# The attention branch placed beside the recurrence's last operations, merged quarters transposed between branch units, and a new prologue

## The reference, cut to what matters

```
h      = rms_norm(x)
proj   = h @ w_in                        # q|k|v, z = r|kr|vr + three low-rank (LORA) pieces, two gates
attn   = sliding_window_attention(q, k, v, sinks)          # 16 heads, window 128
z      = z + (token_shift(z) - z) * shift_mix
y      = rwkv7(z ...)                                      # 16 heads, delta-rule state
y      = (group_norm(y) * ln_w + ln_b + bonus) * g
merged = sigmoid(ga) * (attn @ w_branch_a) + sigmoid(gb) * (y @ w_branch_b)
x      = x + merged @ w_out
x      = x + hierarchical_moe(rms_norm(x))   # 32 experts 2048 -> 512 -> 2048, top 2 of one group
out    = rms_norm(x) * final_norm_w
```

## Time and profile before

| | us |
|---|---|
| median of 3 runs | 1893.07 |
| the profiled execution, device time | 1895.63 |
| its span | 1893.8 |
| PE busy / DVE / ACT / POOL | 1454.5 / 487.2 / 342.5 / 31.8 |

### The profile page before, as it was taken

The page is one execution under the profiler, slowest core; times in us unless marked ns, Lnnn a source line. Parts: engine busy times, 40 slices in busy tenths (PEclk is TensorE's granted clock), DMA queues, the critical chain, the costliest instruction groups (busy, mean ns, idle before and its releaser), DMA issues.

```text
span 1893.8 us, 23945 instructions
## 1 busy us (share of the span) xinstructions
PE 1454.5 (77%) x10765; PEld 834.2 (44%) x10765; DVE 487.2 (26%) x614; ACT 342.5 (18%) x396; POOL 31.8 (2%) x23
## 2 busy tenths in 40 slices
PE   5999999999889979899656657566575675856754
PEld 4999974457546748777411212112121131311311
DVE  2454433352343245544201001001010010100102
ACT  2444422212121123334300001000010000100001
POOL 0000000001001000000000000000000000000000
PEclk9999999899979989999888888778887797887976
DMA  7655433241202247545599999999999999999993
GB/s 229 239 188 188 165 108 122 84 146 51 101 8 99 97 162 238 196 155 207 228 422 421 422 422 422 421 422 422 422 422 422 423 421 423 422 422 422 422 422 145
DMA packets 114683, 529.00 MB, mean 279 GB/s; under 512 B 7729, under 2 KB 9883, under 8 KB 64572
## 3 DMA queue, kind: packets, MB, share of 16 engines
q1 hardware_dynamic: 109184, 512.27, 67.8%
q10 hardware_dynamic: 4284, 11.58, 1.8%
q0 software_dynamic: 1152, 4.19, 0.6%
HBM read 521.74 MB, written 6.29 MB: 279 GB/s over the span
## 4 chain that ended last, share of the span: by engine, by line
PE 58%; DMA 32%; DVE 4%; ACT 3%; issue 1%; ACTq 1%; DVEq 0%; SPq 0%
DMA ring<-in_expert_w_down 21%; DMA ring<-in_expert_w_up 11%; PE ps L469 10%; PE ps L521 10%; PE ps L789 9%; PE ps L890 6%; PE ps L907 5%; PE ps L916 3%; PE ps L859 2%; DMA ring<-in_expert_w_gate 1%; PE ps L433 1%; PE ps L458 1%; PE ps L697 1%; PE ps L680 1%; PE ps L699 1%
## 5 line engine op out<-in xcount | busy, mean ns | idle before, releaser
L890 PE MATMUL ps<-ring,arena 128*32 128x512 f32 x1280 | 178.5, 708 | 101.2 <-DMA ring<-in_expert_w_up 83.1
L521 PE MATMUL ps<-ring,arena 128*128 128x512 f32 x512 | 232.8, 607 | 2.8 <-ACT rs L1070 2.8
L907 PE MATMUL ps<-ring,arena 128*32 128x512 f32 x768 | 134.8, 867 | 83.2 <-DMA ring<-in_expert_w_down 83.2
L890 PE MATMUL ps<-arena 128*32 128x512 f32 x768 | 117.8, 769 | 78.1 <-DMA arena<-in_expert_w_up 42.8
L469 PE MATMUL ps<-h_hi,w_hi 128*128 128x256 f32 x544 | 154.7, 284 | 2.8 <-DVE w_lo L1309 2.8
L469 PE MATMUL ps<-h_lo,w_hi 128*128 128x256 f32 x544 | 154.7, 284 | 0.0
L469 PE MATMUL ps<-h_hi,w_lo 128*128 128x256 f32 x544 | 154.6, 284 | 0.0
L521 PEld LDWEIGHTS ps<-ring,arena 128*128 128x128 f32 x512 | 96.4, 193 | 118.4 <-issue 111.3
L890 PEld LDWEIGHTS ps<-ring,arena 128*32 128x32 f32 x1280 | 45.3, 127 | 220.4 <-issue 121.9
L1675 DVE TENSOR_TENSOR arena<-arena,ps 128x512 f32<-128x512 f32 x64 | 44.0, 687 | 356.0 <-PE ps L916 356.0
L789 PE MATMUL ps<-v_hi,m_hi 128*128 128x512 f32 x256 | 102.5, 400 | 14.5 <-DVE v_lo L1509 9.3
(11 more groups left out here) (265 smaller groups left out, 1585.0 us busy)
## 6 DMA issues: line engine op xcount, KB each, us to landing
ring<-in_expert_w_up SPq DMA_DIRECT2D x24, 4096.0 KB, 24.7
ring<-in_expert_w_down SPq DMA_DIRECT2D x24, 4096.0 KB, 24.3
ring<-in_w_in SPq DMA_DIRECT2D x34, 2048.0 KB, 7.8
arena<-in_expert_w_gate SPq DMA_DIRECT2D x16, 4096.0 KB, 24.2
ring<-in_expert_w_gate SPq DMA_DIRECT2D x16, 4096.0 KB, 22.7
arena<-in_expert_w_up SPq DMA_DIRECT2D x8, 4096.0 KB, 15.1
arena<-in_expert_w_down SPq DMA_DIRECT2D x8, 4096.0 KB, 24.3
ring<-in_w_out SPq DMA_DIRECT2D x8, 2048.0 KB, 7.9
```

Source lines behind the costliest of these rows:

```text
L521: last = mm(ps[:, 7, :], hT[:, k, 128 * t:128 * t + 128], slot(n)[:, k % 8, :], start=k == 0, stop=k == KT - 1)
L890: last = mm(ps[32 * j:32 * j + 32, u % 2, :], XS[:, k, 32 * j:32 * j + 32], w[:, j, kk, :], start=k == 0, stop=k == KT - 1, tile_position= ...
L907: last = mm(ps[32 * j:32 * j + 32, 2 + nb, :], HIDT[:, kh, 32 * j:32 * j + 32], w[:, j, 512 * nb:512 * nb + 512], start=kh == 0, stop=kh == 3,
```

## The change

Seven things are changed.

1. The prologue. SP issues the identity, both halves of x and then the z chunks; the LORA chunks come behind q|k|v. PE transposes raw x as each half lands. `hT` holds x times the norm weight without the 1/rms, which is applied behind the products: DVE multiplies each z and q|k tile with `rbc` (1/rms of each token, spread over partitions by a product of ones and a diagonal), ACT scales v and the gates. x is split in 8 blocks, the first z unit needs 4 of them.
2. The LORA products are 6 units (UL) of 24 matmuls in split precision behind q|k|v, where they were 48 float32 products ahead of z.
3. The constants and eight small transfers move from ACT's queue to POOL's, behind the landing of the first z chunk.
4. The attention branch's units stand on PE right behind the last transposes of y; DVE and ACT prepare their pieces between the last operations of y. The weight pieces have 3 buffers through branches and w_out, where the branches had 4.
5. The merged quarters are transposed and split one at a time, each behind the third unit of the next quarter, into `n_hi`, `n_lo`, a pair of their own; `mg` is gone. The last quarter is transposed behind the third unit of w_out. The gates lie where y was, so POOL fetches them only when y is split (`m_lo_done` 3).
6. x is fetched again by POOL behind the first four gate loads. The first expert unit goes to another place and waits for the branches' last unit.
7. One semaphore counts the products of a half of the recurrence (`half_ps`), where each had one; the order is the same.

```diff
+            over(late, "below_n", [P, 4096], F32)
+            n_hi, n_lo = (over(late, f"n_{x}", [P, KT, TOK]) for x in ("hi", "lo"))
...
-        gates = [[A(LW0 + 1024 * (2 * b + g), 1024).rearrange("p (a n) -> p a n", a=TT) for g in range(2)] for b in range(2)]
-
-        hfn = A(HT, 4096).rearrange("p (a d) -> p a d", a=TT)
+        gates = [[A(8192 + 1024 * (2 * b + g), 1024).rearrange("p (a n) -> p a n", a=TT) for g in range(2)] for b in range(2)]
...
-        UZ, UQ, UM, UO = 48, 24, 32, 32
+        UZ, UQ, UL, UM, UO = 48, 24, 6, 32, 32
...
-            for h in range(2):
-                load(h, slot(h, LORA_W), cols(LORA0, h, LORA_W))
+            xv = a["x"][0].rearrange("(a p) d -> p a d", p=P)
+            sp.dma_start(cst[:, 0:256], a["consts"][:, 0:256]).then_inc(S("ident_in"), 16)
+            for t in range(TT):
+                sp.dma_start(x_raw[:, t, :], xv[:, t, :]).then_inc(S(f"x_in{t}"), 16)
...
+            for h in range(2):
+                load(NL + h, slot(NL + h, LORA_W), cols(LORA0, h, LORA_W))
...
-            sp.wait_ge(S("mg_done"), 4)
-            sp.wait_ge(S("mtr_ps"), 8)
+            sp.wait_ge(S("v_used"), UM)
...
+            pool.wait_ge(S("slot_full0"), 16)
+            pool.dma_start(cst[:, 256:NCONST], a["consts"][:, 256:NCONST]).then_inc(S("const_in"), 16)
+            for dst, src in ((sink[:, :], a["attn_sinks"][0].partition_broadcast(P)), (wua[0:64, :], a["rwkv_w_up"][0]),
+                             (wua[64:128, :], a["rwkv_a_up"][0]), (g1w[:, :], a["rwkv_g_up"][0, 0:128, :]),
+                             (g2w[0:32, :], a["rwkv_g_up"][0, 128:160, :]), (w0row[0:1, :], a["rwkv_w0"]),
+                             (rbias[:, 0:4], a["router_group_b"][0].partition_broadcast(P)),
+                             (rbias[:, 4:36], a["router_expert_b"][0].partition_broadcast(P))):
+                pool.dma_start(dst, src).then_inc(S("small_in"), 16)
...
-            pool.wait_ge(S("y_done"), HALVES)
+            pool.wait_ge(S("m_lo_done"), 3)
...
+                if nb == 2:
+                    pool.dma_start(x_sb[:, :, :], a["x"][0].rearrange("(a p) d -> p a d", p=P)).then_inc(S("x2_in"), 16)
...
-            pe.wait_ge(S("const_in"), 16)
-            pe.wait_ge(S("vec_in"), 16 * 12)
-            tp(ps[:, 0, 0:NVEC], vrow[0:NVEC, :]).then_inc(S("vt_ps"), 1)
-            pe.wait_ge(S("vt_done"), 1)
-            pe.wait_ge(S("xn_done"), 2)
-            transposes(xn, "xt_ps")
-            pe.wait_ge(S("ht_done"), 8)
-
-
-            full(0)
-            full(1)
-            for t, m in enumerate((128, 128, 32)):
-                for k in range(KT):
-                    last = mm(ps[0:m, 4 + t, 0:TOK], slot(k // 8, LORA_W)[:, k % 8, 128 * t:128 * t + m], hT[:, k, :],
-                              start=k == 0, stop=k == KT - 1)
-                    if t == 2 and k % 8 == 7:
-                        last.then_inc(S("chunk_used"), 1)
-                if t < 2:
-                    last.then_inc(S("z_ps"), 1)
+            pe.wait_ge(S("ident_in"), 16)
+            pe.wait_ge(S("anorm_in"), 16)
+            tp(ps[:, 7, 0:16], vrow[0:16, :]).then_inc(S("pro_ps"), 1)
+            for g, (t, kq) in enumerate(BLOCKS):
+                if kq == 0:
+                    pe.wait_ge(S(f"x_in{t}"), 16)
+                if g == 7:
+                    pe.wait_ge(S("pro_dve"), 1)
+                for q in range(4):
+                    k = 4 * kq + q
+                    last = tp(ps[:, g, 128 * q:128 * q + 128], x_raw[:, t, 128 * k:128 * k + 128])
+                last.then_inc(S("xt_ps"), 1)
+            pe.wait_ge(S("ht_done"), 2)
+            pe.wait_ge(S("vec_in"), 16 * 11)
+            tp(ps[:, 0, 0:NVEC], vrow[0:NVEC, :]).then_inc(S("pro_ps"), 1)
+            pe.wait_ge(S("pro_dve"), 1 + TT)
+            for t in range(TT):
+                last = mm(ps[:, 1, 128 * t:128 * t + 128], C("ones"), diag[:, t, :], start=True, stop=True)
+            last.then_inc(S("pro_ps"), 1)
+            pe.wait_ge(S("pro_dve"), 5)
...
+            pe.wait_ge(S("qk_done"), 8)
+            for y in range(UL):
+                h, t = divmod(y, 3)
+                m = (128, 128, 32)[t]
+                pe.wait_ge(S("w_lo"), UZ + UQ + y + 1)
+                for k in range(8):
+                    for p, (w, v) in enumerate(PRODUCTS):
+                        last = mm(ps[0:m, 4 + t, 0:TOK], pieces(q_buffer(UQ + y)[0])[w][:, m * k:m * k + m], hf(v, 8 * h + k),
+                                  start=h == 0 and k == 0 and p == 0, stop=h == 1 and k == 7 and p == 2)
...
-            pe.wait_ge(S("m_lo_done"), 3)
-            with pe.Fori(0, 2) as i:
-                for x in range(16):
-                    c, q = divmod(x, 4)
-                    b, g = divmod(c, 2)
-                    if q == 0:
-
-                        pe.wait_ge(S(("m1_done", "m2_done")[g]), i * 2 + (b + 1))
-                    pe.wait_ge(S("v_lo"), i * 16 + (x + 1))
-                    late_unit(x % 4, 2 * g, range(8 - 8 * g + 2 * q, 8 - 8 * g + 2 * q + 2), q == 0, q == 3)
-            pe.wait_ge(S("mg_done"), 4)
-            transposes(mg, "mtr_ps")
-            pe.wait_ge(S("m_lo_done"), 3 + 8)
+            def n_transposes(nb):
+
+                pe.wait_ge(S("mg_done"), nb + 1)
+                if nb >= 2:
+                    pe.wait_ge(S("n_lo_done"), TT * (nb - 1))
+                for t in range(TT):
+                    for q in range(4):
+                        last = tp(ps[:, 4 + 2 * (nb % 2) + t, 128 * q:128 * q + 128],
+                                  gates[nb % 2][0][:, t, 128 * q:128 * q + 128])
+                    last.then_inc(S("mtr_ps"), 1)
+
+            pe.wait_ge(S("m_lo_done"), 1)
+            for y in range(UM):
+                c, q = divmod(y, 4)
+                nb, g = divmod(c, 2)
+                if y == 4:
+                    pe.wait_ge(S("m_lo_done"), 3)
+                if q == 0 and nb:
+                    pe.wait_ge(S(("m1_done", "m2_done")[g]), nb)
+                pe.wait_ge(S("v_lo"), y + 1)
+                late_unit((m_hi, m_lo), y % 3, 2 - 2 * g, range(8 - 8 * g + 2 * q, 8 - 8 * g + 2 * q + 2), q == 0, q == 3)
+                if y > 8 and y % 8 == 2:
+                    n_transposes(y // 8 - 1)
...
+                if x < 8 and x % 2 == 0:
+                    pe.wait_ge(S("n_lo_done"), TT * (x // 2 + 1))
                 pe.wait_ge(S("v_lo"), UM + x + 1)
-                late_unit(x % 3, 2 * nb, range(8 * h + 2 * q, 8 * h + 2 * q + 2), h == 0 and q == 0, h == 1 and q == 3)
+                late_unit((n_hi, n_lo), (UM + x) % 3, OUT_BANK[nb], range(8 * h + 2 * q, 8 * h + 2 * q + 2), h == 0 and q == 0, h == 1 and q == 3)
+                if x == 2:
+                    n_transposes(3)
...
-            squares(x_sb, junk, "ss_done")
+                f(junk[:, t, :], x_raw[:, t, :], ACT.Square, accum_out=rstd[:, t:t + 1]).then_inc(S("ss_done"), 1)
+                for g in range(2 * t, 2 * t + 2):
+                    h_split(g)
...
+            h_split(4)
+            h_split(5)
+            z_hi(0, 0)
+            h_split(6)
+            h_split(7)
+            z_hi(1, 0)
+            z_hi(2, 0)
...
+                    v_hi(0)
                     f(m_hi[:, 0:4, :], yT[:, 0:4, :], ACT.Copy).then_inc(S("m_hi_done"), 1)
+                    v_hi(1)
+                    v_hi(2)
...
+            def n_hi_out(nb):
+
+                for t in range(TT):
+                    o, i = n_block(nb, t)
+                    act.wait_ge(S("mtr_ps"), TT * nb + t + 1)
+                    f(n_hi[o], i, ACT.Copy).then_inc(S("n_hi_done"), 1)
...
+            def h_out(g):
+                dve.wait_ge(S("xt_ps"), g + 1)
+                v.tensor_tensor(hT[block(g)], ps[:, g, :].rearrange("p (k t) -> p k t", k=4),
+                                rep(vec("anorm", 4 * BLOCKS[g][1], 4), 128), ALU.mult).then_inc(S("ht_done"), 1)
+
+            def h_rest(g):
+                dve.wait_ge(S("h_hi_done"), g + 1)
+                dve.wait_ge(S("ht_done"), g + 1)
+                v.tensor_tensor(h_lo[block(g)], hT[block(g)], h_hi[block(g)].bitcast(F32), ALU.subtract)\
+                    .then_inc(S("h_lo_done"), 1)
...
+            def z_mul(e, i):
+                c = 4 * (e // 8) + e % 4
+                dve.wait_ge(S("w_used"), i * 16 + (4 + e + 1))
+                v.tensor_tensor(zs[:, c % 4, :], ps[:, c, 0:TOK], rbc[:, :], ALU.mult).then_inc(S("zs_done"), 1)
...
-                    for h, (dst, src) in enumerate(((slice(8, 16), attnT), (slice(0, 4), yT[:, 0:4, :]))):
-                        dve.wait_ge(S("m_hi_done"), h + 1)
-                        v.tensor_tensor(m_lo[:, dst, :], src, m_hi[:, dst, :].bitcast(F32), ALU.subtract)\
-                            .then_inc(S("m_lo_done"), 1)
-                dve.wait_ge(S("ynt_ps"), hh + 1)
+                    m_rest(slice(8, 16), attnT, 1)
+                    v_lo(0)
+                dve.wait_ge(S("half_ps"), half_at("ynt", hh))
                 for j in range(HJ):
```

(49 more changed lines are left out.)

434 lines of the change are left out of this document (220 added, 214 removed).

## The result

The changed kernel takes 1861.2 us, the median of 4 runs (1857.94 to 1865.21), against 1893.13 for the kernel before beside it (1892.5 to 1894.77): a ratio of 0.9831, interval [0.981, 0.9852]. The forecast was 1859.1, in a range of 1852 to 1871. The span of the profiled execution is 1860.0 us, 33.8 less than before, where 34.0 were forecast. A second measurement (first experiment) gives 1860.93.

The account below looks back on a forecast made before the run. The fixed-length expert weight stream starts when w_out ends, so earlier gains pass on one to one. Prologue and LORA 14.0, end of the recurrence 9.3, branches to w_out 10.7: 34.0 off 1893.1 gives 1859.1 us, range 1852 to 1871.

Parts of the forecast that it names:

- What bounds the kernel: The expert weight stream has fixed length from SP's fourth expert issue, so gains or losses ahead pass on one to one.
- One sign: The stretch between attention and the end of the recurrence keeps its length; another length would make the forecast wrong.
- Prologue, 31.1: Start of z: first unit at 21.2 us, units following as if from 22.7 instead of 53.85, gaining 31.1 us.
- the step named: In the prologue, the second weight piece waits for blocks 6 and 7 and is ready at 25.4 us.
- The lower bound: First z chunk lands at 14 to 15 us, ahead of the need at 18.9; the upper bound was 27.2.
- LORA, 17.3: Behind q|k|v: 6 LORA units of 2.88 us each cost 17.3 us.
- The softmax, 0.6: Attention's first softmax: DVE has two more operations ahead of it and PE waits for its end, 0.6 us lost.
- The end of the recurrence, 9.3: Branch units start while y is still being prepared; unit 3 ends at 710.2 instead of 719.5, gaining 9.3 us.
- Between branches and w_out, 10.7: The 11.49 us gap and 2.7 of slow clock go, 3.5 of transposes stay: 10.7 us gained.
- Late weights: Rival (0.14): in the prologue the first z chunk lands at 27 us instead of 15; gain 26 us, time 1867.
- leaking overlap: Rival (0.12): gates land late (3 us) and waits between units 0 to 3 bring the slow clock (3 more); 1865.
- The slow level: Rival (0.04): short waits for weight pieces keep PE at the lower clock level through branches and w_out; time 1994.

Follow-up runs that it names:

- first experiment: The changed kernel once more, unaltered, as the base for the other runs: 1860.93 us (also written experiment 1).
- Experiments 2 and 3: Kernel before with only the new prologue and LORA: 1880.54 us; kernel before with only the new end (attention branch first, merged quarters one at a time): 1874.12 us.
- experiment 8: Changed kernel with POOL's nine transfers of constants and small matrices (1.9 MB) issued at once, not behind the first z chunk's landing: 1867.39 us.
- experiment 4: Changed kernel, but PE starts the first branch unit only when all of the left side, y too, is split: 1871.74 us.
- Experiment 5: Changed kernel, but the last merged quarter is transposed and split ahead of w_out's first unit instead of behind its third: 1871.59 us.

## Why the prediction was right

- **What bounds the kernel.** Right, and the claim on which all else rests: the stretch of the experts kept its length and speed, and SP's fourth issue moved by 33.13 us for 33.8 of span. Experiments 2 and 3 add up for the same reason. The length is fixed to some 3 us, not better: over the twelve profiled executions 959.6 to 962.7 us follow the fourth issue, and 33.8 to 35.4 lie between the third and the fourth. The other signs came too, or nearly: first z product at 20.53 (21 to 22), third z unit at 28.60 (about 28), first branch product at 683.69 (near 683), last weight product at 1826.60. One sign fails by its letter: from the first scores to the transposes ahead of the branches it is 433.2 us before (261.99 to 695.15), 434.5 in the changed kernel and 431.9 in experiment 1, so this length moves from run to run by more than the forecast allowed.
- **Prologue, 31.1.** Forecast: first product at 21.2, units as if from 22.7. Measured: 20.53 and, with LORA's start at 230.20 less 207.4, 22.8. What sets it is not the step named, though: the second piece is ready at 24.5 (23.32 + 1.2), not 25.4, and the second unit starts at 25.7, when the first has come through the lower level (0.53 in 20.53:26.00). The two lie 1.2 us apart, so that 22.7 came out is luck. The working also slips: its terms from 16.9 on add to 20.9 and 25.0, where it has 21.2 and 25.4. Measured, blocks 4 and 5 are scaled from 16.11 on, and the first product follows 4.4 us later. ACT's table load at 6.00 (6.1), the z chunk landed by 15.13 (14 to 15). The lower bound for that landing was the right one because the change also holds 1.9 MB back; experiment 8 shows 6.5 us without.
- **LORA, 17.3.** Measured 247.35 - 230.20 = 17.15. Scores at 247.3 against 247.7.
- **The softmax, 0.6.** The wait was sized right: PE's idle there is 2.38 us, where it was 1.88 before the change, so 0.5 more. What the forecast put at nothing is the clock behind it. In the profiled execution it falls: the transposes take 1.94 us instead of 1.06. Ahead of this place the execution is 0.3 us behind that of experiment 1 (first scores at 247.28 against 247.01), behind it 1.9 (second scores at 269.14 against 267.27), so 1.6 us are lost. In experiment 1 it holds and costs nothing. The branches start 2.9 us later than there; the rest comes from later slow stretches that last longer (clock 0.76 in 544:552 against 0.90 in the same place of experiment 1, and 0.79 in 632:640 against 1.00).
- **The end of the recurrence, 9.3.** Units 2 and 3 start at 690.07 and 693.56. Forecast: 703.7 and 707.4 less 14.0, that is 689.7 and 693.4. The waits between units, 0.47 to 0.81 us, did not bring the clock down: 1.00 in 682.60:693.56. Without the units there (experiment 4) 10.8 us are lost. The gates, issued at 692.66, landed in 4.4 to 10.1 us and cost PE nothing. POOL's four issues took 722 to 762 ns while DVE formed three weight remainders (692.28 to 696.00). The 3100 ns that the Trainium skill ("SBUF — State Buffer", section "SBUF: two separate sides") gives are those of a transfer beside a copy on VectorE; an operation with two inputs in the on-chip memory, as these remainders are, it counts only against a POOL operation that reads there. So the forecast had applied the figure to operations that it is not about, and the 722 ns don't speak against the section.
- **Between branches and w_out, 10.7.** From unit 3 to w_out's end it takes 178.89 us (872.45 - 693.56). The forecast had 61 units of 2.72, 3.5 of transposes and 8.2 of other work: 177.6, 1.3 too few, which is not placed. Experiment 5 loses 10.7.
- **The sum.** w_out ends 32.6 us earlier, not 34.0; 1.2 come back between there and the end. So the span agrees to 0.2 us because two small errors cancel and by the choice of execution: the spans of the four runs lie between 1856.2 and 1863.4. The medians give 31.9 and 33.4, which is what the 34.0 is to be held against.
- **The rivals.** Late weights and leaking overlap did not come about, but late landings of either kind cost time, and each is a step away: 6.5 us with the constants ahead, 8.5 with x ahead of the gates. The slow level did not stay: 806 matmuls and transposes from 693.56 to 872.45 run at 1.00 (the two windows of the result).

## What to carry to other kernels

First find the stage of fixed length and its trigger; everything ahead of it then adds up in microseconds, part by part. A wait of some microseconds on TensorE can cost twice, once as idle time and once in the clock behind it, so a gap is closed only when its last quarter is, and independent matmuls belong ahead of such a wait. Transfers that nobody needs yet are held back until the first one that PE waits for has landed.
